# Block state space and attention divided behind its values, in the second mixer of a two-layer block on one Trainium2 core

## The chip, the core and the metric

One core of one Trainium2 chip runs the whole program in one launch. The metric is the device time of one execution in microseconds (us). TensorE (PE), VectorE (DVE), ScalarE (ACT), GpSimd (POOL) and SyncE (SP) run their own instruction lists side by side and wait for each other on semaphores.

## The reference, cut to what matters

`first_block` has two layers, each a mixer and a SwiGLU network; `second_block` follows with two more layers. Everything is float32 on 256 tokens of width 1024. The change is in `first_block`: mostly in layer 1's mixer (`odd_mixer`), which runs a diagonal state space on 256 of its 1024 inner channels (16 groups of 16 channels, 64 complex states a group) beside an attention with 6 heads of width 128.

```python
def s5_ssm(u, a_re, a_im, log_dt, b_re, b_im, c_re, c_im, d_skip, w_glu, b_glu):
    mag = exp(lr * dt); ab = mag * (cos(li * dt) + i sin(li * dt))   # 16 x 64 states
    bu = einsum('bsgh,gph->bsgp', ug, bb)                # drive: complex, 16 -> 64 a group
    x = associative_scan(x[t] = ab * x[t-1] + bu[t])     # over the 256 tokens
    y = einsum(x_re, c_re) - einsum(x_im, c_im) + d_skip * ug
    z = gelu(y)
    return z * sigmoid(z @ w_glu + b_glu)
def mla_attention(...):                                  # 6 heads, causal by chunks of 64
    p = softmax(where(mask, q . k * scale, -inf))        # blocks of 128 queries
    return einsum('bhqk,bkhd->bqhd', p, v)
def odd_mixer(t, ...):
    proj = t @ w_in
    return concatenate([s5_ssm(...), mla_attention(...)]) @ w_out
```

## The kernel before, in words

**Weights.** Every large product is done three times: a weight chunk (128 x 1024 float32, two DMAs of 256 KB by SP into `raw`) is rounded by ACT to `wh` (line 865), POOL forms the rest `wl` in two halves (lines 787, 788), and PE multiplies `wh` by the rounded activations `xh`, `wh` by their rest `xl`, and `wl` by `xh` (lines 2411 to 2413). `raw`, `wh` and `wl` are rings of 6 slots; SP may refill a slot when its chunk is used. The chunks of `w_mod` (the modulation of `second_block`) go straight from `raw` into PE: 8 instructions on four column strips of 32 each (line 2516). They are laid between the steps of `first_block` as `modulate(...)`; twelve pairs stand in the attention loop.

**Order.** Each engine's list is written out by hand; the code's order is the order of the engine. A float32 product leaves two records in the trace, a transpose one.

**First mixer.** DVE's `angles()` reduces the states' angles to one turn (`reduced`, 5 or so small instructions a call) and raises `disc_v`; ACT's exponential (line 1142) waits for it, with attention and convolution queued behind. `discretise()` follows. `state_tables()` makes full tables on DVE in pieces (`yield`) that the first feed-forward network takes between its own instructions: the scaled input matrices, and cosine and sine of every state at each of the 256 tokens.

**Second mixer, PE.** `modulate("mod1_in")` and the turns of the normalised rows (`rows_turn`, line 2574); tile in1; turns of the input matrices (`b_turn`, line 2550) and of u (256 channels by tokens, `ssm_ut`); latent turns (line 2890); the projections uq and ukv with the first drives and states between them; turns of q and k (line 2945; three of them wait for the rotation, `mla_rope`); then the attention loop.

**State space.** The 1024 complex states stand in 8 tiles j of 128. `drive(j)` is two products of 128 x 256 (line 2862), into a bank that DVE multiplies by cosine and sine, scans over 256 tokens and turns back (`state_space`, lines 2017 to 2038); for j of 3 and up POOL does the additions and the turning back. `state(j)` is two products 128 x 256 (line 2870) that add up in one bank; line 2091 adds the skip, ACT takes gelu.

**Attention loop.** Unit u is query block u % 2 of head u // 2. PE: scores of u + 2 (lines 2964, 2965), two modulation chunks, wait `at_p`, one or two transposes of p (line 2986), a drive or a state at odd u, and for odd u from 3 the values of head u // 2 - 1 (lines 2972, 2973), which wait `at_y`, the last head having left `mla_out`. DVE: reciprocal of the row sum (line 2079), maximum of the next unit, and the split of the head's output into `xh` and `xl` (lines 1467, 1469). ACT: p times the reciprocal (line 1275), evacuation of the transposes (line 1281), next exponential (line 1267). Behind the loop stand the values of head 5, `state(7)` and the products of out1 (line 2411).

Of the kernel before, what the change touches and what calls it, by code (L numbers as in the profile page):

```python
# [34 lines left out]
SSM_C, SSM_T, SSM_J = D // 4, (D // 4) // P, 8  # L35
MH, MN, MR, MV = 6, 128, 64, 128
# [8 lines left out]
       ("ln_g", CONV_T), ("ln_b", CONV_T), ("b_glu", SSM_T), ("d_skip", SSM_T), ("a_re", SSM_J), ("a_im", SSM_J),  # L45
# [4 lines left out]
       ("cos_d", 64), ("sin_d", 64), ("cos_x", 64), ("sin_x", 64), ("modsum", 48), ("count", 16)]  # L50
# [23 lines left out]
def constants():  # L74
# [14 lines left out]
    put("count", np.broadcast_to(np.arange(16), (P, 16)))  # L89

# [18 lines left out]
def lay_out(x):  # L109
# [14 lines left out]
    v["b_glu"], v["d_skip"] = cols(x["l1_b_glu"]), cols(x["l1_d_skip"])  # L124
# [10 lines left out]
    def blocks(a):  # L135
        a = np.asarray(a)
        out = np.zeros((2, 64, SSM_J, P), f)
        for g in range(16):
            at = 16 * (g % 8)
            out[g % 2, :, g // 2, at:at + 16] = a[g]  # L140
        return out.reshape(P, SSM_J * P)
# [10 lines left out]
        "b_re": blocks(x["l1_b_re"]), "b_im": blocks(x["l1_b_im"]),  # L152
        "c_re": blocks(np.asarray(x["l1_c_re"]).transpose(0, 2, 1)),
        "c_im": blocks(np.asarray(x["l1_c_im"]).transpose(0, 2, 1)),
# [82 lines left out]
def build(nc, a, out):  # L237
# [61 lines left out]
    POOL_STATES = 3  # L299
# [14 lines left out]
    with ExitStack() as stack:  # L314
# [36 lines left out]
        def view(phase, *shape, at=None):  # L351
# [12 lines left out]
        pc, ps_ = view("ssm", SSM_J, SEQ), view("ssm", SSM_J, SEQ)  # L364
# [19 lines left out]
        bbar = [view("l0", SSM_J, P, at=KEEP + 7296 + i * 1024) for i in range(2)]  # L384
        braw = [view("l0", SSM_J, P, at=KEEP + 4096 + i * 1024) for i in range(2)]
        btmp = [view("l0", SSM_J, P, at=KEEP + 3072), view("l0", SSM_J, P, at=KEEP + 6144)]
        ptmp = view("l0", SSM_J, SEQ, at=KEEP + 4096)
        angle, sin_half, sin_n, cos_n = (bt[0].rearrange("p a b -> p (a b)")[:, 256 * i:256 * i + 256]
                                         .rearrange("p (j n) -> p j n", j=SSM_J) for i in range(4))
        turns_f = bt[1].rearrange("p a b -> p (a b)")[:, 0:256].rearrange("p (j n) -> p j n", j=SSM_J)  # L390
        turns_i = bt[1].rearrange("p a b -> p (a b)")[:, 256:512].rearrange("p (j n) -> p j n", j=SSM_J).bitcast(I32)
# [385 lines left out]
        def _(pool):  # L777
# [20 lines left out]
            def state(j):  # L798
# [4 lines left out]
                if j > POOL_STATES:  # L803
                    pool.wait_ge(x_state, j + j - POOL_STATES)
# [2439 lines left out]
```

## Time and profile before

| | |
|---|---|
| timed executions | 1824.0, 1834.28, 1822.65 us; median 1824.0 |
| profiled execution | 1826.6 us, span 1824.8 us |
| PE busy | 1779.4 us, 98% |
| POOL busy | 1376.5 us, 75% |
| ACT, DVE busy | 903.2 us, 804.2 us |
| DMA moved | 348.28 MB, mean 191 GB/s |
| first feed-forward network | about 130 to 326 us of the span |
| second mixer | about 326 to 453 us, its attention loop 384 to 422 |

Idle time in brackets is that of the engine just before the instruction, with what ended it. Ends of products are modelled, so a PE row may overlap the next: prices come from the chain of waits or from distances of starts.

### The profile page before, as it was taken

The page shows a single profiled execution, that of the slowest core. Times are in us where ns is not written, and L with a number is a line of the kernel's source. Part 1 is how long each engine was busy: PE and PEld are TensorE (multiplying, and loading weights), DVE is VectorE, ACT ScalarE, POOL GpSimd, SP SyncE. Part 2 cuts the span into 40 slices and gives each one's busy share as a digit, 9 for nine tenths or more (in the row PEclk, how much of TensorE's full clock was granted, in tenths as well). Part 3 has the DMA queues.
Part 4 walks back from the last instruction along what each step waited for, and adds up shares of the span by engine and source line. Part 5 has one row for each costly group of instructions (what it writes and reads, how often), then busy time and mean ns, then how long its engine had stood idle before and what let it go on. Part 6 is the DMA issues. An engine that isn't in the chain of part 4 may idle for free.

```text
span 1824.8 us, 28994 instructions
## 1 busy us (share of the span) xinstructions
PE 1779.4 (98%) x9846; PEld 1442.8 (79%) x9846; DVE 804.2 (44%) x1556; ACT 903.2 (49%) x1410; POOL 1376.5 (75%) x811
## 2 busy tenths in 40 slices
PE   9989999998999999999999999999999999999997
PEld 7768888766788887788888977788888987788886
DVE  4565874573455554443112555441114665441112
ACT  6456443645644554555445445554446445554443
POOL 7359997546988779578888884578887894678884
PEclk9999999999999999999999999999999999999999
DMA  7767876688987745346665562356654563346562
GB/s 271 192 196 255 274 245 217 193 280 272 294 273 249 234 139 185 115 137 194 199 189 181 168 190 93 120 158 201 201 184 150 171 209 107 110 148 194 189 189 70
DMA packets 259110, 348.28 MB, mean 191 GB/s; under 512 B 20936, under 2 KB 161608, under 8 KB 259016
## 3 DMA queue, kind: packets, MB, share of 16 engines
q1 hardware_dynamic: 255840, 340.44, 58.4%
q10 hardware_dynamic: 3176, 6.62, 1.3%
q8 instruction: 55, 0.90, 0.2%
q14 instruction: 39, 0.32, 0.1%
HBM read 343.24 MB, written 1.64 MB: 189 GB/s over the span
## 4 chain that ended last, share of the span: by engine, by line
PE 88%; DVE 5%; ACT 2%; issue 1%; DMA 1%; POOL 1%; SPq 0%; DVEq 0%; POOLq 0%; ACTq 0%
PE bank L2411 23%; PE bank L2413 23%; PE bank L2412 22%; PE bank L2550 2%; PE bank L3128 2%; PE bank L2481 1%; PE bank L2480 1%; PE bank L2479 1%; PE bank L3118 1%; PE bank L3167 1%; PE bank L2516 1%; POOL wl L828 1%; PE bank L2783 1%; PE bank L2574 0%; ACT wh L865 0%
## 5 line engine op out<-in xcount | busy, mean ns | idle before, releaser
L828 POOL TENSOR_TENSOR wl<-raw,wh 128x1024 fp32r<-128x1024 f32 x300 | 734.1, 2461 | 102.5 <-ACT wh L1030 79.0
L2411 PE MATMUL bank<-wh,xh 128*128 128x512 f32 (+1 forms) x1590 | 625.4, 393 | 9.6 <-POOL wl L788 2.9
L2413 PE MATMUL bank<-wl,xh 128*128 128x512 f32 (+1 forms) x1590 | 611.4, 385 | 0.0
L2412 PE MATMUL bank<-wh,xl 128*128 128x512 f32 (+1 forms) x1590 | 609.9, 384 | 0.0
L787 POOL TENSOR_TENSOR wl<-raw,wh 128x512 fp32r<-128x512 f32 (+1 forms) x232 | 309.5, 1334 | 286.0 <-ACT wh L865 284.5
L1030 ACT ACTIVATE wh<-raw 128x1024 fp32r<-128x1024 f32 x270 | 286.4, 1062 | 429.0 <-PE bank L2413 411.9
L865 ACT ACTIVATE wh<-raw 128x1024 fp32r<-128x1024 f32 (+2 forms) x268 | 275.6, 1049 | 170.7 <-PE bank L2413 90.1
L2411 PEld LDWEIGHTS bank<-wh,xh 128*128 128x128 f32 x1590 | 299.1, 188 | 73.8 <-issue 8.2
L2413 PEld LDWEIGHTS bank<-wl,xh 128*128 128x128 f32 x1590 | 298.7, 188 | 60.8
L2412 PEld LDWEIGHTS bank<-wh,xl 128*128 128x128 f32 x1590 | 299.5, 188 | 54.8
L788 POOL TENSOR_TENSOR wl<-raw,wh 128x512 fp32r<-128x512 f32 (+1 forms) x232 | 309.6, 1335 | 0.0
L1599 DVE TENSOR_TENSOR arena<-arena,bank 128x256 f32<-128x256 f32 x66 | 24.8, 418 | 323.2 <-ACT arena L1017 323.2
L2411 PE MATMUL bank<-wh,hh 128*128 128x512 f32 x420 | 163.6, 389 | 0.0
L2413 PE MATMUL bank<-wl,hh 128*128 128x512 f32 x420 | 163.5, 389 | 0.0
L2412 PE MATMUL bank<-wh,hl 128*128 128x512 f32 x420 | 163.4, 389 | 0.0
L1602 DVE CAST hh<-bank 128x512 fp32r<-128x512 f32 x55 | 38.0, 691 | 189.8 <-PE bank L2550 189.8
L1923 DVE SCALAR_TENSOR_TENSOR bank<-arena,small,bank 128x256 f32<-128x256 f32 x216 | 86.9, 481 | 11.1 <-DMA arena<-in_w_mod 11.1
L2413 PEld LDWEIGHTS bank<-wl,hh 128*128 128x128 f32 x420 | 78.9, 188 | 16.4
L2412 PEld LDWEIGHTS bank<-wh,hl 128*128 128x128 f32 x420 | 78.9, 188 | 16.3
L2411 PEld LDWEIGHTS bank<-wh,hh 128*128 128x128 f32 x420 | 78.8, 188 | 16.3
L1391 ACT ACTIVATE arena<-bank 128x256 f32<-128x256 f32 (+2 forms) x96 | 41.9, 490 | 97.7 <-PE bank L3128 97.7
L2272 DVE TENSOR_REDUCE small<-bank 128x1 f32<-128x256 f32 (+2 forms) x96 | 50.5, 554 | 82.3 <-PE bank L3118 81.2
(399 smaller groups left out, 2037.3 us busy)
## 6 DMA issues: line engine op xcount, KB each, us to landing
raw<-in_w_ffn_in SPq DMA_DIRECT2D x264, 256.0 KB, 2.9
raw<-in_w_in SPq DMA_DIRECT2D x224, 256.0 KB, 2.9
raw<-in_w_ffn_out SPq DMA_DIRECT2D x132, 256.0 KB, 2.9
raw<-in_w_mod SPq DMA_DIRECT2D x120, 256.0 KB, 4.3
raw<-in_l_w_gate SPq DMA_DIRECT2D x88, 256.0 KB, 3.7
raw<-in_l_w_up SPq DMA_DIRECT2D x88, 256.0 KB, 4.4
raw<-in_l_w_down SPq DMA_DIRECT2D x88, 256.0 KB, 4.1
arena<-in_w_mod SPq DMA_DIRECT2D x36, 512.0 KB, 5.4
```

Of the source, the lines that this page charges most:

```text
L787: nc.gpsimd.tensor_tensor(wl[:, s, 0:h], raw[:, s, 0:h], words(wh)[:, s, 0:h], ALU.subtract)
L788: nc.gpsimd.tensor_tensor(wl[:, s, h:n], raw[:, s, h:n], words(wh)[:, s, h:n], ALU.subtract)\
L828: nc.gpsimd.tensor_tensor(wl[:, s, :], raw[:, s, :], words(wh)[:, s, :], ALU.subtract)\
L865: nc.scalar.activation(wh[:, s, first:n], raw[:, s, first:n], ACT.Copy).then_inc(hi_ready, 1)
L1030: nc.scalar.activation(wh[:, s, :], raw[:, s, :], ACT.Copy).then_inc(hi_ready, 1)
L1391: nc.scalar.activation(pT2[:, e, 0:keys // P, (i % 2) * P:(i % 2) * P + P], unit_bank(u)[:, 0:keys].rearrange("p (a b) -> p a b", b=P), AC ...
L1602: v.tensor_copy(hh[:, :, :], src).then_inc(hid_split, 1)
L1923: ins = v.scalar_tensor_tensor(out=dst, in0=raw_mod[:, k, :], scalar=c, in1=acc, op0=ALU.mult, op1=ALU.add)
L2272: v.tensor_reduce(nmax[:, g % 4:g % 4 + 1], unit_bank(u)[:, 0:keys], AX_X, ALU.max, negate=True)\
L2411: mm(dst, x_hi, w_hi, start=first, stop=False, skip_group_check=True)
L2412: mm(dst, x_lo, w_hi, start=False, stop=False, skip_group_check=True)
L2413: return mm(dst, x_hi, w_lo, start=False, stop=last, skip_group_check=True)
```

## The change

The state space goes over blocks of 4 tokens (`SSM_L`), 64 blocks. Within a block, outputs come from a 128 x 128 matrix for each 32 channels (`near`: powers of the state's factor between B and C, plus the skip), made on PE in 32 x 128 pieces (`near_products`) and completed on DVE (`near_matrix`). Between blocks, B times the powers 3 to 0 (`bpow`) drives one complex state a block; DVE scans 64 blocks for four tiles at once, 256 columns, and C times the powers 1 to 4 (`cpow`) reads it. So there are two calls c = 0, 1 of `drive`, `state` and the DVE chain instead of eight, none of it on POOL. `block_rows` lays u out by place in the block, in place of its four transposes. Inputs `ssm_b`, `ssm_c` (as many bytes as b_re and b_im had) come over ACT's queue; SP's loads of c_re and c_im (512 KB each), with SP's waits for `res_done` and `mod_acc` ahead of in1, are gone.

Attention: p is no longer scaled. The reciprocals of a head's sums are spread over 128 rows by two transposes in `mla_values`; ACT copies the raw output to `q1` (`mla_raw`), DVE multiplies and splits (`mla_divided`).

First mixer: `angles()` reduces one angle more, makes three products of angles, 12 exponents a state and the denominators; ACT's exponential has 96 columns for 8. `step_factors()` (20 or so small instructions) goes behind the copy of the modulation rows, and `state_tables()` has ten pieces.

On PE this is one odd step of the attention loop (u = 3; from its modulation chunks to the next unit's scores), before:

```order
L2516 MATMUL bank<-raw,cw 32x256 x8
L2986 MATMUL bank<-con,arena 128x128 x2
L2862 MATMUL bank<-Y,arena 128x256 x2
L2870 MATMUL bank<-extra,arena 128x256 x2
L2972 MATMUL bank<-arena 128x256
L2973 MATMUL bank<-arena 128x128
```

and now:

```order
L2549 MATMUL bank<-raw,cw 32x256 x8
L3049 MATMUL bank<-con,arena 128x128 x2
L3036 MATMUL bank<-con,small 128x128 x2
L3038 MATMUL bank<-arena 128x256
L3039 MATMUL bank<-arena 128x128
```

The drive (2862) and the state (2870) have left the step, and two transposes of reciprocals (3036) have come in ahead of the values.

PE from the last chunk ahead of the turns of q and k to the turns that wait for the rotation, before:

```order
L2516 MATMUL bank<-raw,cw 32x256 x4
L2862 MATMUL bank<-Y,arena 128x256 x2
L2870 MATMUL bank<-extra,arena 128x256 x2
L2945 MATMUL bank<-con,arena 128x128 x12
L2945 MATMUL bank<-con,Y 128x128 x12
L2516 MATMUL bank<-raw,cw 32x256 x12
L2945 MATMUL bank<-con,xf 128x128 x6
```

and now:

```order
L2549 MATMUL bank<-raw,cw 32x256 x4
L3006 MATMUL bank<-con,arena 128x128 x12
L3006 MATMUL bank<-con,Y 128x128 x12
L2549 MATMUL bank<-raw,cw 32x256 x12
L2931 MATMUL bank<-Y,arena 32x64 x4
L2936 MATMUL bank<-extra,arena 32x63 x8
L2931 MATMUL bank<-Y,arena 32x64 x4
L2936 MATMUL bank<-extra,arena 32x63 x8
L2931 MATMUL bank<-Y,arena 32x64 x4
L2936 MATMUL bank<-extra,arena 32x63 x8
```

`drive(3)` and `state(1)` are gone ahead of the turns; the new `state(0)` (2931, 2936) stands behind them (a fourth such round follows, then the turns from `xf`).

ACT at the end of the loop, from the last two units' p to the gelu, before:

```order
L1275 ACTIVATE arena<-arena,small 128x128
L1281 ACTIVATE arena<-bank 128x128
L1275 ACTIVATE arena<-arena,small 128x256
L1281 ACTIVATE arena<-bank 128x2x128
L865 ACTIVATE wh<-raw 128x1024 x3
L1289 ACT_TABLE_LOAD
L1289 ACTIVATE extra<-extra 128x512
```

and now:

```order
L1254 ACTIVATE arena<-bank 128x256
L1264 ACTIVATE arena<-bank 128x128
L1264 ACTIVATE arena<-bank 128x2x128
L1254 ACTIVATE arena<-bank 128x256 x2
L847 ACTIVATE wh<-raw 128x1024 x3
L1276 ACT_TABLE_LOAD
L1276 ACTIVATE extra<-bank 128x4x64 x2
```

The scalings (1275) are gone; the copies of heads 4 and 5 (1254 x2) now stand ahead of the first casts of out1's weights (847).

```diff
-            nc.scalar.activation(mag, t8a, ACT.Exp).then_inc(disc_a, 1)
+            nc.scalar.activation(mag_pow, mag_arg, ACT.Exp).then_inc(disc_a, 1)
...
-            for i, w in enumerate(("b_re", "b_im")):
-                act.dma_start(braw[i], a[w].rearrange("p (j c) -> p j c", j=SSM_J)).then_inc(b_in, 16)
+            for dst, w in ((b_raw, "ssm_b"), (c_raw, "ssm_c")):
+                act.dma_start(dst, a[w].rearrange("p (n j c) -> p n j c", n=2, j=2 * SSM_J)).then_inc(b_in, 16)
...
+            def mla_raw(h):
+                act.wait_ge(at_pv, h + 1)
+                nc.scalar.activation(q1[:, 0, 0:SEQ], mla_out[:, 0:SEQ], ACT.Copy).then_inc(y_raw, 1)
             mla_exp(0)
...
                                      bank[u % 3][:, 0:n * P].rearrange("p (a b) -> p a b", a=n), ACT.Copy).then_inc(at_ev, 1)
                 if u + 2 < 2 * MH:
                     mla_exp(u + 2)
+                if u >= 3 and u % 2:
+                    mla_raw(h - 1)
+            mla_raw(MH - 1)
...
             hi_until(plan.first["out1"] + RING - 1)
-            act.wait_ge(y_skip, 1)
-            nc.scalar.activation(zv, yv, ACT.Gelu_apprx_tanh).then_inc(z_gelu, 1)
+            act.wait_ge(y_state, SSM_T)
+            for c in range(SSM_T):
+                ins = nc.scalar.activation(zv[:, SEQ * c:SEQ * c + SEQ].rearrange("p (b r) -> p r b", r=SSM_L),
+                                           state_bank[:, SEQ * c:SEQ * c + SEQ].rearrange("p (r b) -> p r b", r=SSM_L),
+                                           ACT.Gelu_apprx_tanh)
+            ins.then_inc(z_gelu, 1)
...
-                step(v.tensor_scalar(th16, th, 16.0, None, ALU.mult))
-                settle()
-                reduced(th16, ki, kf)
-                n = spread(C_("count").unsqueeze(1), SSM_J, 16)
-                step(v.tensor_tensor(angle[:, :, 0:16], n, spread(th.unsqueeze(2), SSM_J, 16), ALU.mult))
-                step(v.tensor_tensor(angle[:, :, 16:], n, spread(th16.unsqueeze(2), SSM_J, 16), ALU.mult))
+                step(v.tensor_scalar(th4, th, float(SSM_L), None, ALU.mult))
+                step(v.tensor_scalar(th64, th, 16.0 * SSM_L, None, ALU.mult))
+                settle()
+                reduced(th4, ki, kf)
+                reduced(th64, ki, kf)
+                for at, n, x, by in ((0, 16, th4, "count"), (16, 4, th64, "count"), (20, 12, th, "powers")):
+                    step(v.tensor_tensor(angle[:, :, at:at + n], spread(C_(by)[:, 0:n].unsqueeze(1), SSM_J, n),
+                                         spread(x.unsqueeze(2), SSM_J, n), ALU.mult))
                 settle()
                 reduced(angle, turns_i, turns_f)
+                step(v.tensor_tensor(mag_arg, spread(C_("powers").unsqueeze(1), SSM_J, 12), spread(t8a.unsqueeze(2), SSM_J, 12), ALU.mult))
                 v.tensor_scalar(angle, angle, 3.1415925, -3.1415925, ALU.min, ALU.max).then_inc(disc_v, 1)
...
+            def step_factors():
...
+            def block_decay(c):
+                by_block = decay.rearrange("p (j b) -> p j b", j=4)
+                step(v.tensor_copy(by_block, spread(mag4[:, 4 * c:4 * c + 4].unsqueeze(2), 4, SSM_N)))
+                settle()
+                step(v.memset(by_block[:, :, 0:1], 0.0))
+            def near_matrix(c):
+                dve.wait_ge(near_mm, c + 1)
+                for jj in range(4):
+                    j = 4 * c + jj
+                    ins = v.scalar_tensor_tensor(out=near[:, j, :], in0=ident, scalar=V_("d_skip", j), in1=scratch[:, P * jj:P * jj + P],
+                                                 op0=ALU.mult, op1=ALU.add)
+                    ins.then_inc(near_set, 1) if jj == 3 else step(ins)
...
             undivided_norm("mix1", "l1_mix_pre", accb)
+            near_matrix(0)
+            block_decay(0)
             take("in1", 0, lambda t, p: v.tensor_scalar(proj[:, t, 0:512], p, back[:, t:t + 1], None, ALU.mult))
...
+            near_matrix(1)
...
-                for j in range(SSM_J):
-                    dve.wait_ge(bu_done, j + 1)
-                    b = drive_bank[j % 2]
-                    cosj, sinj = pc[:, j, :], ps_[:, j, :]
+                for c in range(SSM_T):
+                    dve.wait_ge(bu_done, c + 1)
...
-                        n = j - POOL_STATES
-                        if n:
-                            dve.wait_ge(x_scan, 2 * n)
-                        v.tensor_tensor(two(spun), two(b[:, :]), cos2, ALU.mult).then_inc(bu_taken, 1)
-                        v.tensor_tensor(two(turned), two(b[:, :]), sin2, ALU.mult).then_inc(bu_taken, 1)
-                        yield
...
                     step(v.tensor_tensor(two(spun), two(b[:, :]), cos2, ALU.mult))
                     step(v.tensor_tensor(scanned[:, 0:SEQ], b[:, SEQ:], sinj, ALU.mult))
-                    v.tensor_tensor(scanned[:, SEQ:], b[:, 0:SEQ], sinj, ALU.mult).then_inc(bu_taken, 1)
+                    step(v.tensor_tensor(scanned[:, SEQ:], b[:, 0:SEQ], sinj, ALU.mult))
...
-            for _ in range(5):
+            for _ in range(2):
...
             v.engine_nop().then_inc(mla_rope, 1)
-            for _ in range(3):
-                next(ssm)
...
+            def mla_divided(h):
+                y = mla_out[:, 0:SEQ]
+                dve.wait_ge(y_raw, h + 1)
+                step(v.tensor_tensor(y, q1[:, 0, 0:SEQ], mla_out[:, SEQ:], ALU.mult))
+                settle()
+                split(2 + h, 1, y, at_y)
...
                 v.reciprocal(rinv[:, u % 4:u % 4 + 1], rsum[:, u % 4:u % 4 + 1]).then_inc(at_rinv, 1)
...
+                next(ssm, None)
                 if u >= 3 and u % 2:
                     h = u // 2 - 1
-                    dve.wait_ge(at_pv, h + 1)
-                    split(2 + h, 1, mla_out[:, 0:SEQ], at_y)
...
+            mla_divided(MH - 1)
...
-            ahead_of_norm("mod1_in", "mix1")
+            def near_products(c):
+                if c:
+                    pe.wait_ge(near_set, c)
+                for j in range(4 * c, 4 * c + 4):
+                    for i in range(2):
+                        for q in range(SSM_L):
+                            ins = mm(scratch[32 * q:32 * q + 32, P * (j % 4):P * (j % 4) + P], bpow[i][:, j, SSM_L - 1, :],
+                                     cpow[i][:, j, 3 - q:7 - q, :].rearrange("p d c -> p (d c)"), start=i == 0, stop=i == 1,
+                                     skip_group_check=True)
+                ins.then_inc(near_mm, 1)
+            modulate("mod1_in", slice(0, 2))
+            pe.wait_ge(b_bar, 1)
+            pe.wait_ge(c_pow, 1)
+            near_products(0)
+            rows_turn("mix1", (0, 1))
...
+            def block_rows():
+                for j in range(SSM_J):
+                    for t in range(TT):
+                        at = SSM_N * j + 32 * t
+                        for q in range(SSM_L):
+                            ins = mm(ut_bank[32 * q:32 * q + 32, at:at + 32], proj[:, t, SSM_G * j:SSM_G * j + SSM_G],
+                                     ident.rearrange("p (b s) -> p s b", s=SSM_L)[:, q, :], start=True, stop=True, skip_group_check=True)
+                ins.then_inc(ssm_ut, 1)
+            def drive(c):
+                for jj in range(4):
+                    for i in range(2):
+                        at = SEQ * i + SSM_N * jj
+                        ins = mm(drive_bank[c][:, at:at + SSM_N], bt[i][:, 4 * c + jj, :], uT1[:, c, SSM_N * jj:SSM_N * jj + SSM_N],
+                                 start=True, stop=True, skip_group_check=True)
                 ins.then_inc(bu_done, 1)
-            def state(j):
-                pe.wait_ge(x_state, j + 1 + max(0, j + 1 - POOL_STATES))
-                y = state_bank[:, SEQ * (j // 4):SEQ * (j // 4) + SEQ]
-                for i in range(2):
-                    ins = mm(y, cz[i][:, j, :], z_cos[:, SEQ * i:SEQ * i + SEQ], start=j == 0 and i == 0, stop=j % 4 == 3 and i == 1,
-                             skip_group_check=True)
+            def state(c):
+                pe.wait_ge(near_set, c + 1)
+                pe.wait_ge(x_state, c + 1)
+                for r in range(SSM_L):
+                    at = SEQ * c + SSM_N * r
+                    for jj in range(4):
+                        mm(state_bank[32 * jj:32 * jj + 32, at:at + SSM_N], near[:, 4 * c + jj, SSM_G * r:SSM_G * r + SSM_G],
+                           uT1[:, c, SSM_N * jj:SSM_N * jj + SSM_N], start=True, stop=False, skip_group_check=True)
+                    for i in range(2):
+                        for jj in range(4):
+                            z = SEQ * i + SSM_N * jj
+                            ins = mm(state_bank[32 * jj:32 * jj + 32, at + 1:at + SSM_N], cpow[i][:, 4 * c + jj, 4 + r, :],
+                                     z_cos[:, z:z + SSM_N - 1], start=False, stop=i == 1, skip_group_check=True)
                 ins.then_inc(y_state, 1)
...
+            near_products(1)
+            for b in range(2):
...
+            block_rows()
...
-            state(1)
...
+            state(0)
...
+                pe.wait_ge(at_rinv, 2 * h + 2)
+                for qb in range(2):
+                    at = (2 * h + qb) % 4
+                    tr(mla_out[:, SEQ + qb * P:SEQ + qb * P + P], rinv[:, at:at + 1].broadcast_to([P, P]), ident)
...
-            drive(4)
-            state(2)
-            drive_at, state_at = {1: 5, 3: 6, 5: 7}, {3: 3, 5: 4, 7: 5, 9: 6}
...
-                pe.wait_ge(at_p, u + 1)
+                pe.wait_ge(at_exp, u + 1)
                 for kc in range(1 + u % 2):
...
-                if u in state_at:
-                    state(state_at[u])
+                if u == 6:
+                    state(1)
                 if u >= 3 and u % 2:
...
-            state(7)
```

## Rows read from the trace of the kernel before

**Rows 1.** The page: busy time, share of the span, instructions; chain by engine.
```profile
PE 1779.4 (98%) x9846; PEld 1442.8 (79%) x9846; DVE 804.2 (44%) x1556; ACT 903.2 (49%) x1410; POOL 1376.5 (75%) x811
```

**Rows 2.** Windows: engines busy in each stretch, PEclk, DMA share, GB/s.
```profile
130.00:326.00 196.00, 193.87 (x948) 158.24 (x938) 123.71 (x215) 90.83 (x119) 176.21 (x73) 1.00 0.73 239
...
381.00:424.00 43.00, 37.88 (x319) 24.59 (x317) 29.36 (x75) 16.34 (x51) 29.73 (x37) 1.00 0.87 296
```

**Rows 3.** DVE, ACT, PE timelines, first mixer: start, us, instruction [idle<-releaser].
```profile
83.55 0.57 DVE L1660 SCALAR_TENSOR_TENSOR small<-small 128x8 f32<-128x8 f32 x3
84.15 0.29 DVE L1675 TENSOR_TENSOR arena<-con,small 128x128 f32<-128x128 f32 x1
...
86.72 0.29 DVE L1679 TENSOR_SCALAR arena<-arena 128x256 f32<-128x256 f32 x1
...
87.89 0.22 ACT L1142 ACTIVATE small<-small 128x8 f32<-128x8 f32 x1
...
95.96 1.09 PE L2550 MATMUL bank<-con,arena 128*128 128x128 f32 x8 [0.85 <-DVE arena L1876]
```

**Rows 4.** Chain of waits: start, us, engine, line; PE prices.
```profile
332.71 0.87 PE bank L2574 x8
...
388.08 1.00 PE bank L2516 x16
...
389.45 0.87 PE bank L2862 x4
```

**Rows 5.** Groups of lines, PE: form, records | busy us, mean ns | idle before.
```profile
L3144 PE MATMUL bank<-arena 128*64 128x64 f32 x128 | 5.1, 222 | 0.0
L2542 PE MATMUL bank<-con,rdiag 128*128 128x24 f32 x32 | 3.9, 258 | 0.0
```

**Rows 6.** PE timeline, second mixer: waits of the block state space.
```profile
327.59 1.09 PE L2574 MATMUL bank<-con,X 128*128 128x128 f32 x8 [2.01 <-DVE X L1558]
...
347.04 0.66 PE L2890 MATMUL bank<-con,arena 128*128 128x128 f32 x4 [0.86 <-DVE arena L1979]
...
372.86 1.47 PE L2945 MATMUL bank<-con,arena 128*128 128x128 f32 x12
...
378.12 0.88 PE L2945 MATMUL bank<-con,xf 128*128 128x128 f32 x6 [1.05 <-DVEq L2064]
...
383.75 1.13 PE L2870 MATMUL bank<-extra,arena 128*128 128x256 f32 x4 [1.01 <-DVE extra L2038]
...
386.95 0.70 PE L2964 MATMUL bank<-arena 128*128 128x256 f32 x2 [0.37 <-ACT arena L1281]
...
418.20 0.33 PE L2986 MATMUL bank<-con,arena 128*128 128x128 f32 x1 [0.48 <-ACT arena L1275]
```

**Rows 7.** ACT timeline: last evacuation of the value projection.
```profile
371.37 0.41 ACT L1255 ACTIVATE arena<-bank 128x256 f32<-128x256 f32 x1
```

**Rows 8.** Windows inside the attention loop: DMA share and GB/s.
```profile
415.00:420.00 5.00, 4.52 (x47) 2.86 (x46) 2.41 (x8) 2.09 (x7) 3.88 (x5) 1.00 0.98 341
```

**Rows 9.** PE, ACT, DVE, POOL timelines at the end of the loop.
```profile
419.46 0.44 PE L2986 MATMUL bank<-con,arena 128*128 128x128 f32 x2
419.73 0.60 PE L2972 MATMUL bank<-arena 128*128 128x256 f32 x2
...
420.21 1.05 ACT L865 ACTIVATE wh<-raw 128x1024 fp32r<-128x1024 f32 x1
...
420.59 0.42 DVE L1467 CAST xh<-bank 128x256 fp32r<-128x256 f32 x1 [2.82 <-PE bank L2973]
...
422.63 1.27 POOL L788 TENSOR_TENSOR wl<-raw,wh 128x512 fp32r<-128x512 f32 x1
```

**Rows 10.** Chain of waits: first product of the output GEMM.
```profile
424.04 0.47 PE bank L2411
```

**Rows 11.** Windows around the one stretch at the lower clock.
```profile
104.00:107.50 3.50, 1.62 (x8) 1.00 (x6) 0.00 (x0) 2.00 (x2) 1.76 (x2) 1.00 1.04 383
107.50:111.00 3.50, 3.48 (x9) 2.77 (x10) 0.00 (x0) 0.00 (x0) 1.59 (x2) 0.54 0.92 334
```

More of the change, by code:

```diff
@@ L383, in build @@
         u_copy = nc.dram_tensor("u_copy", (2, 32, 4, 2, PAD + SEQ + 1), F32, kind="Internal").ap()
[L384 to L389, printed above, removed]
@@ L1738, in state_tables @@
                 yield
                 settle()
-                step(v.tensor_tensor(pc, pc, ptmp, ALU.subtract))
+                v.tensor_tensor(bpow_all, bpow_all, t, ALU.add).then_inc(b_bar, 1)
                 yield
-                step(v.tensor_tensor(four(ps_), coarse(sin_n), fine(cos_n), ALU.mult))
-                settle()
+                dve.wait_ge(b_bar, 1)
+                c_far, t = cpow_all[:, :, SSM_L:], blocks(c_tmp, SSM_L)
+                step(v.tensor_tensor(c_far, each(c_raw[:, 0], SSM_L, SSM_G), factors(c_re, SSM_L, SSM_G), ALU.mult))
@@ L2853, in _ @@
             pe.wait_ge(mod_ready, 8)
-            ahead_of_norm("mod1_in", "mix1")
-            def b_turn(b):
-                turn(b_bank[b], lambda i, t: bbar[i][:, 2 * b + t, :], b_tr)
-            def drive(j):
-                if j >= 2:
-                    pe.wait_ge(bu_taken, j - 1 + max(0, j - 1 - POOL_STATES))
-                for i in range(2):
-                    ins = mm(drive_bank[j % 2][:, SEQ * i:SEQ * i + SEQ], bt[i][:, j, :], uT1[:, j // 4, :], start=True, stop=True,
-                             skip_group_check=True)
-                ins.then_inc(bu_done, 1)
@@ L2878, in _ @@
             column_tile("in1", 0, 0, "mix1", rest_of_rows)
-            pe.wait_ge(b_bar, 2)
-            for b in range(3):
+            near_products(1)
+            for b in range(2):
                 b_turn(b)
             tile_chunk("in1", 1, 0)
-            pe.wait_ge(b_ev, 2)
-            b_turn(3)
+            for b in range(2, 4):
+                pe.wait_ge(b_ev, 2 * b - 2)
+                b_turn(b)
             def latent_turn(i):
@@ L2913, in _ @@
             latent_chunk("uq", 2)
-            drive(2)
             x_ready("lat1", 2)
@@ L2918, in _ @@
                 latent_chunk("ukv", i, shift=2)
-                if i == 0:
-                    pe.wait_ge(c_neg, 1)
-                    pe.wait_ge(c_in, 32)
-                    state(0)
-            drive(3)
-            state(1)
             def mla_turn(b):
```

225 lines of the change are left out of this document (114 added, 111 removed).

## The prediction

> **What bounds the kernel now.** The page first [rows 1]: PE is busy for 98% of the span, so only what PE does or waits for is worth anything. The windows [rows 2] (start and end, length, then busy time of PE, PEld, DVE, ACT and POOL with their counts, granted clock, DMA share, GB/s) show where it waits: of the 196 us of the first feed-forward network PE misses 2, of the 43 us of the attention loop 5. All the change's work on POOL, and nearly all on DVE, therefore moves under PE. The first mixer, the second mixer's PE list and the seam between loop and out1 can move the end.
>
> **First mixer.** In `angles()` three of five small instructions of a reduction take 0.57 [rows 3], so one more reduction costs 0.95; with one scaling more (0.19), a third product of angles and the exponents (0.29 at most each, the product of 128 columns) it ends some 1.5 later than 86.72 + 0.29: at 88.5. ACT's exponential started at 87.89 and had waited for nothing, so it comes 0.6 later; 96 columns for 8 cost 0.1 at most. PE waits 0.85 at 95.96 for the DVE work behind that, so I pass the delay on: **+0.6** (bounds 0, if slack on the way takes it, and 1.5). `step_factors()`, 20 instructions of 0.19, is 3.8 us of DVE beside a feed-forward network in which DVE is busy 124 of 196 [rows 2]; the tables there shrink a little. Both 0; were they on the path, 3.8.
>
> **PE's products.** Prices [rows 4, 5]: a drive or a state of before (4 records) takes 0.87; eight transposes 0.87, so 0.11 each; sixteen records on four strips, two rounds of 256 columns, take 1.00, so a round of 128 columns is 0.25 by halving. A round of 64 columns is between 0.125 (halving again) and 0.16 (L3144: 128 records on two strips, 32 rounds, in 5.1 us): I take 0.13. A round of 32 columns lies between 0.0625 and 0.16: 0.1. A product with full 128-column weights and few columns is between 0.11 (a quarter of 0.434) and 0.24 (L2542: 16 instructions in 3.9): I take 0.24, for its shape is nearest.
>
> Removed up to the last transposes of the loop (419.46): 8 drives and 7 states, 13.0, and 4 transposes of u, 0.44. Added: `near_products(1)`, 8 rounds, 2.0; `block_rows`, 16 rounds of 32 columns, 1.6; two drives of 8 products, 3.8; two states of 12 rounds, 3.2; the reciprocals of heads 0 to 3, 8 transposes, 0.87. That is 11.5 (with the rounds and drives at their bounds 8.7 and 13.1): **-2.0**. `near_products(0)`, also 2.0, stands where PE waits 2.01 for DVE at 327.59 [rows 6]: 0; without that cover 2.0.
>
> **PE's waits** [rows 6], each less what now stands ahead of it. The 0.86 at 347.04 is filled by near(1), whose 2.0 I have counted: -0.86. The 1.05 at 378.12: DVE did the chains of three states ahead of the rotation and now does one: -1.05. The 1.01 at 383.75 is for state(2), which is gone: -1.01. The 0.48 at 418.20 is for ACT's scaling, which is gone: -0.48. Waits like the 0.37 at 386.95 stand at the even units; that of the unit behind state(1) is covered: -0.37. Against this, two covers go. The turns at 372.86 had drive(3) and state(1) ahead of them (1.74), while ACT's last copy of the value projection ended at 371.37 + 0.41 = 371.78 [rows 7]; PE would now be there at 371.0: +0.79. At u = 1 no drive covers the softmax any more; of its 0.87 I let half come back: +0.46. Sum of waits **-2.5** (bounds -3.8 and -1.0).
>
> **Supply.** The loop's 24 modulation chunks, less the 6 that the ring holds, are 18 x 0.52 = 9.4 MB; at the 341 GB/s of a window with DMA share 0.98 [rows 8] 27.7 us. PE went from 383.75 to 419.46, 35.7 us, and would now need about 29. Other transfers take a share too, so supply may come out up to 2 short; but 383 GB/s has been seen [rows 11], which would need 24.6. I take **+1.0** (0 to 2.0).
>
> **The seam.** Before [rows 9, 10]: last transposes 419.46, values of head 4 419.73, DVE's cast 420.59, ACT's first cast of out1 420.21, and its first product at 424.04, 3.83 behind that cast (1.05 on ACT, two halves of 1.27 on POOL, hand-overs). All that is 4.58. Now ACT's list has the copies of heads 4 and 5 ahead of the cast, and head 5's needs head 4's split. From the last transposes: values of head 4 end 1.13 later, plus 0.22 of reciprocals, 1.35; ACT copy 0.41 [rows 7] with hand-over, 1.8; multiply, cast, subtract on DVE at 0.46 apiece, 3.2; reciprocals and values of head 5, 1.1, 4.3; its copy, 4.8; then the 3.83: 8.6. So out1 starts **+4.1** later against the last transposes (bounds +2.5, if POOL's lateness is made up in out1's first tile, and +4.6). Queued behind ACT's copy are all casts of out1's chunks, behind those POOL.
>
> **Clock.** PE was busy 1.62 of 3.5 us ahead of 107.5, and in the next 3.5 us the granted clock was 0.54, i.e. 1.2 GHz nearly throughout [rows 11], which costs up to 3.5 x 0.46 = 1.6. In the new seam PE has about 2 of work in 8.6. I expect a fall, partly over idle time: **+1.2** (0 to 1.6).
>
> **Rule against rows.** The trace shows 40 ns a record where 64 columns go over two strips [rows 5] and nothing narrower. The Trainium skill (TensorEngine Tiling (Array Packing), Instruction Overhead) says that a product of one column lasts as long as one of 60, and that nothing is gained by splitting what is already small; (TensorE: Matmul & The Clock Gate, Wait, 56ns, not 53.3ns?) puts a floor of 25 ns between two starts. By it the 128 records of `block_rows` would be an estimated 3.2 for my 1.6 and the 96 of each state 2.4 for 1.6, in all +3.2; no row shows it.
>
> **Sum.** -2.0 - 2.5 + 1.0 + 0.6 + 4.1 + 1.2 = +2.4. The profiled execution took 1826.6 (span 1824.8), so one like it would take 1829.0; it was 2.6 above the median 1824.0 of the timed runs, which is what the forecast is compared with: **1826.4**. With every term at its low bound at once it would be 1818, with every one at its high bound 1832; the forecast's own range is 1821 to 1831.
>
> **Rivals.**
> B, the seam does not grow: POOL and ACT make up their lateness, or the clock stays up. For it: POOL is idle in part [rows 2] and out1's first tile has a modulation chunk between its pieces. Against: the orders are fixed lists, and one head's copy needs the previous head's split. Then -4.5 + 0.6 = -3.9: 1820. Chance 0.2.
> C, small products and supply cost their upper bounds: rounds at 0.16 (+0.7 for the states' 24, +1.0 for the rows' 16), supply 2.0 for 1.0, clock 1.6 for 1.2, waits 0.8 worse: +3.9 on the forecast, so 1830. For it the 0.16 of L3144 and the DMA share of 0.98. Against: 383 GB/s is possible. Chance 0.28.
> D, the other side: strips do not overlap for short products, and each of the 224 small instructions (32 + 32 + 64 + 96) costs 0.24 as one of L2542. That is 53.8 - 2.0 of cover against my 6.8: +45, so 1871. It decides (over 1% slower, 1842) from 0.11 an instruction. Against: L2516 does 8 of 256 columns on four strips in 1.00. Chance 0.04.
> E, the SSM's gain is eaten anyway: DVE's chain for 256 columns is late at state(0) or state(1), each up to 1.0 (the wait of state(2) before). 1828. Chance 0.06.
>
> **How the numbers follow.** Forecast 0.42, B 0.2, C 0.28, E 0.06, D 0.04. About 1% is what a measurement of this kernel can tell from no change: 18 us. Only D is beyond it: slower 0.05. Nothing here can give 18 us, since the whole second mixer's SSM is 13: faster 0.01. The range 1818 to 1834 holds B and C with the spread of single runs.
>
> **What would show it.** Right: state(2)'s and the rotation's waits gone; POOL without `z_cos` work; a new wait of 1.8 or so ahead of the last head's values and one of over 3 ahead of out1's first product; ACT's first cast of out1 over 4 behind the last transposes; granted clock under 1 there; the exponential of the first mixer at 88.5. Wrong: `block_rows` over 3 us, a state over 3, DMA waits of the loop's chunks over 2 us, out1's first product within 6 us of the last transposes, or new waits of b-table turns behind near(1).

## The result

| | before | changed |
|---|---|---|
| timed executions | 20: median 1822.99 us, 1821.06 to 1834.28 | 20: median 1832.09 us, 1825.71 to 1838.46 |
| ratio to before | | 1.0037, 95% interval 1.0024 to 1.005 |
| profiled execution | 1826.6 us, span 1824.8 us | 1828.23 us, span 1826.4 us |

The change makes the kernel slower by 0.24 to 0.5%, some 4 to 9 us; forecast was +2.4. The medians lie 9.1 us apart. The ratio is smaller: it is near that of the means (1.0038), and four of before's 20 executions, at 1831 or more, raise before's mean. The two profiled spans differ by 1.6 only. Two things hide the rest. The profile of before holds a stretch at half clock [rows 11] and a late load in its first mixer; run e4 below keeps the first mixer of before and has neither, so they vary between executions. And the profile of the changed kernel is free of a stall that three more profiles with the same state space will show (e1, e2, f1), and that, by the spread of the times, most of its executions seem to have. The spread is part of the result: the changed kernel's executions cover 13 us.

The late load is in ACT's timeline of the first mixer, first of before, then of the changed kernel:

```profile
105.47 1.06 ACT L865 ACTIVATE wh<-raw 128x1024 fp32r<-128x1024 f32 x1 [3.21 <-DMA raw<-in_l_w_out]
```

```profile
104.05 1.06 ACT L847 ACTIVATE wh<-raw 128x1024 fp32r<-128x1024 f32 x1 [1.15 <-DMA raw<-in_l_w_out]
```

ACT's cast of a chunk of out0 waits for its load in both and comes 1.4 us later in the profile of before (105.47 for 104.05). With the half clock behind it, 1.7 us, this makes 3.1 of the 3.2 us that the changed kernel's profile gains between 100 and 111 us. Another 0.9 us goes the other way later: at 505.98 PE waits 1.38 us for DVE, in before 0.47, and DVE stands behind loads of `w_mod`. This wait is 0.87 in e1 and absent in f1 and f2, so it too varies between executions, and nothing here was run on it.

**The page and the windows of the changed kernel**, answering [rows 1, 2] (window, length, then busy time of PE, PEld, DVE, ACT, POOL with their counts, granted clock, DMA share, GB/s):

```profile
PE 1781.3 (98%) x10270; PEld 1445.5 (79%) x10270; DVE 794.8 (44%) x1568; ACT 900.1 (49%) x1404; POOL 1346.8 (74%) x776
```

```profile
130.00:326.00 196.00, 194.82 (x1000) 159.85 (x996) 128.56 (x233) 90.28 (x118) 172.90 (x74) 1.00 0.73 235
...
381.00:424.00 43.00, 34.41 (x391) 21.84 (x390) 19.46 (x65) 16.80 (x48) 5.95 (x5) 0.95 0.90 318
424.00:453.00 29.00, 27.17 (x147) 19.23 (x145) 6.55 (x11) 13.15 (x22) 14.78 (x13) 0.96 0.63 207
```

PE is about as busy as before (1781.3 us for 1779.4), with 424 records more. POOL's 29.73 us in the loop's window are 5.95 now. The granted clock of 0.95 in the loop's window is new: in [rows 2] it is 1.00.

**PE's timeline of the changed kernel in the second mixer** (start, busy us, instruction; in brackets idle time ahead of it and what ended it), answering [rows 6]:

```profile
322.73 1.93 PE L2893 MATMUL bank<-arena 128*32 128x128 f32 x64
324.91 1.09 PE L2607 MATMUL bank<-con,X 128*128 128x128 f32 x8 [0.26 <-DVE X L1548]
...
339.00 1.95 PE L2893 MATMUL bank<-arena 128*32 128x128 f32 x64
...
345.88 2.12 PE L2913 MATMUL bank<-con,arena 128*32 128x32 f32 x128
...
352.21 2.00 PE L2921 MATMUL bank<-Y,arena 128*128 128x64 f32 x16
...
371.87 1.53 PE L3006 MATMUL bank<-con,arena 128*128 128x128 f32 x12 [0.73 <-ACT arena L1236]
...
375.95 0.30 PE L2931 MATMUL bank<-Y,arena 128*32 128x64 f32 x8
...
377.40 0.87 PE L3006 MATMUL bank<-con,xf 128*128 128x128 f32 x6
...
386.19 0.49 PE L3026 MATMUL bank<-arena 128*128 128x128 f32 x2 [0.47 <-ACT arena L1264]
```

Lines 2893 (`near_products`), 2913 (`block_rows`), 2921 (drive) and 2931 (the first of a state's four rounds) are the new products. `near_products(0)` fits into the old wait of 2.01 and leaves 0.26 of it. The waits of 0.86 at the latent turns, 1.05 at the rotation and 1.01 at a state are gone; 0.73 at 371.87 and 0.47 at 386.19 are the two covers that went.

**The seam in the changed kernel**, PE and ACT, answering [rows 9, 10]:

```profile
411.70 0.64 PE L2549 MATMUL bank<-raw,cw 128*32 128x256 f32 x8 [0.60 <-DMA raw<-in_w_mod]
412.27 0.44 PE L3049 MATMUL bank<-con,arena 128*128 128x128 f32 x2
...
412.76 0.60 PE L3038 MATMUL bank<-arena 128*128 128x256 f32 x2
...
415.48 0.40 PE L3036 MATMUL bank<-con,small 128*128 128x128 f32 x2 [1.90 <-issue]
...
420.69 0.76 PE L2444 MATMUL bank<-wh,xh 128*128 128x512 f32 x1 [4.15 <-POOL wl L798]
```

```profile
413.62 0.38 ACT L1254 ACTIVATE arena<-bank 128x256 f32<-128x256 f32 x1 [0.49 <-PE bank L3039]
416.58 0.38 ACT L1254 ACTIVATE arena<-bank 128x256 f32<-128x256 f32 x1 [2.58 <-PE bank L3039]
416.86 1.99 ACT L847 ACTIVATE wh<-raw 128x1024 fp32r<-128x1024 f32 x2
```

Last transposes at 412.27, the values of head 4 at 412.76, ACT's copy of head 4 at 413.62, of head 5 at 416.58, only then the first cast of out1, and its first product at 420.69: 8.42 us behind the transposes for 4.58 before, with PE idle 1.90 and 4.15. The clock answers:

```profile
419.30:426.20 6.90, 5.51 (x16) 3.93 (x20) 0.00 (x0) 3.45 (x4) 6.19 (x6) 0.51 0.24 83
453.40:456.90 3.50, 3.50 (x25) 1.81 (x22) 2.97 (x5) 3.45 (x6) 3.25 (x4) 0.51 0.89 250
```

In the first window PE's work on the first quarter of out1's tile and the modulation chunk behind it goes from 420.69 to 426.66, 5.97 us; before it went from 424.04 to 427.53, 3.49 us. The low clock costs 2.5 us there. The second window stands behind a wait of PE of 1.83 us at the start of the second feed-forward network, which before had as well, at the full clock; it costs 1.0 us more.

### The profile page after: what moved, and what is told of

It reads as the page before. It is cut to its first block, busy times and chain, and to the rows that moved or that the text cites. A ratio compares the mean times of both kernels' runs of the same rounds, so it can differ in the third digit from the quotient of the medians.

```text
span 1826.4 us, 29796 instructions
## 1 busy us (share of the span) xinstructions
PE 1781.3 (98%) x10270; PEld 1445.5 (79%) x10270; DVE 794.8 (44%) x1568; ACT 900.1 (49%) x1404; POOL 1346.8 (74%) x776
## 4 chain that ended last, share of the span: by engine, by line
PE 88%; DVE 4%; ACT 3%; POOL 1%; issue 1%; DMA 1%; SPq 0%; ACTq 0%; POOLq 0%; DVEq 0%
PE bank L2444 23%; PE bank L2446 23%; PE bank L2445 23%; PE bank L2583 3%; PE bank L3188 2%; PE bank L2514 1%; PE bank L2513 1%; PE bank L2512 1%; PE bank L3178 1%; PE bank L3227 1%; PE bank L2549 1%; POOL wl L810 1%; PE bank L2607 1%; DVE X L1548 0%; ACT wh L847 0%
```

## The experiments

Beside these runs the kernel before had medians of 1824.17 (31 executions, runs e1 to e4) and 1823.63 us (35 executions, runs f1 to f4). Runs of different groups are best compared by their distance from these.

### e1_after_again: the changed kernel once more

> The changed kernel once more, for a second profile and a second comparison with the kernel before. Two theories run through these runs. Theory S (seam): what costs is the end of the attention loop, where ACT's copies of heads 4 and 5 stand ahead of the first casts of out1 (first product 8.4 us behind the last transposes instead of 4.6), and the granted clock falls in the idle time there; the block state space itself gains about 4.5. Theory B (blocks): the block state space costs in most executions, by its many short products or by the longer start in the first mixer, and the seam is a minor matter. Both expect here 1829 to 1833 us, 6 to 9 over the kernel before. S: a stretch at half clock behind the seam in this profile too, the interval from last transposes to out1's first product 8.4. B: low clock or lost time also in the first mixer or around the short products.

Median 1833.79 us (1826.25 to 1842.66, 9 executions), ratio 1.005 (1.0029 to 1.0071), 0.8 above the range that both theories gave. The seam was as in the first profile, 8.42 us from the last transposes (418.94) to out1's first product (427.36), with a stretch at half clock behind it; out1's first quarter took 5.40 us. The low stretch at 453 is missing here, though the wait of 1.83 ahead of it is not. But this span is 1831.1, and a second stretch stands at 155, behind a stop of PE that neither theory had:

```profile
157.29 1.11 PE L2583 MATMUL bank<-con,arena 128*128 128x128 f32 x4 [4.38 <-DVE arena L1586]
```

```profile
155.00:161.90 6.90, 4.61 (x13) 3.83 (x14) 5.59 (x14) 2.95 (x3) 3.54 (x3) 0.51 0.37 130
424.60:431.40 6.80, 4.04 (x10) 3.20 (x11) 0.41 (x1) 4.39 (x5) 6.68 (x6) 0.50 0.38 133
```

PE waits 4.38 us for DVE early in the first feed-forward network. DVE comes out of `step_factors()`, 18 small instructions. These are its rows and POOL's at that time:

```profile
142.19 1.31 DVE L1722 TENSOR_TENSOR arena<-arena,small 128x32 f32<-128x32 f32 x1
...
146.03 2.30 DVE L1727 COPY arena<-arena 128x32 f32<-128x32 f32 x1
148.25 2.44 DVE L1712 TENSOR_SCALAR arena<-arena 128x32 f32<-128x32 f32 x1
150.61 2.43 DVE L1730 COPY arena<-arena 128x32 f32<-128x32 f32 x1
152.96 2.38 DVE L1712 TENSOR_SCALAR arena<-arena 128x32 f32<-128x32 f32 x1
155.26 0.17 DVE L1730 COPY arena<-arena 128x32 f32<-128x32 f32 x1
```

```profile
144.66 1.29 POOL L798 TENSOR_TENSOR wl<-raw,wh 128x512 fp32r<-128x512 f32 x1
145.91 9.40 POOL L810 TENSOR_TENSOR wl<-raw,wh 128x1024 fp32r<-128x1024 f32 x4
```

An instruction on 128 x 32 numbers takes 1.2 to 1.3 us, then 2.3 to 2.4. POOL's rows are halves of chunks of 1.28 and, in one row of four, whole chunks of 9.40 / 4 = 2.35, starting at 145.91, 148.26, 150.61 and 152.96. DVE's slow instructions start at 146.03, 148.25, 150.61 and 152.96 and end with them; when POOL pauses at 155.31, the next takes 0.17. In the first profile of the changed kernel the longest of the 18 are the last two:

```profile
146.25 4.89 DVE L1733 COPY arena<-arena 128x256 f32<-128x256 f32 x2
```

So in the two profiles DVE and POOL interleave differently: the 18 instructions took 10.8 us in the first profile of the changed kernel (140.37 to 151.14), 15.5 here (140.42 to 155.91), and 3.4 would be 18 of 0.19. The slack that hides them ends near 151, so the first case costs nothing and the second 4.7 us and, with the clock that falls in the stop, some 6.5: the offset between the two profiles is 0 up to 149 us and 6.5 at 162.

### e2_casts_first: out1's first casts ahead of the raw copies

```diff
+                if u == 2 * MH - 1:
+                    hi_until(plan.first["out1"] + 1)
                 if u >= 3 and u % 2:
                     mla_raw(h - 1)
+            hi_until(plan.first["out1"] + 3)
             mla_raw(MH - 1)
```

> The changed kernel with ACT's cast of out1's first chunk ahead of the copy of head 4, and two more casts ahead of the copy of head 5; nothing else moved. Theory S: out1's first product comes 4.7 to 5.5 us behind the last transposes instead of 8.4, no idle stretch over 2.5 us in the seam, so 3 to 3.5 less idle and 2.5 less at half clock: 1823 to 1826 us. Theory B: 1828 to 1831, since at best the 3.5 of the seam come back.

Median 1826.81 us (1820.77 to 1831.14, 12 executions), ratio 1.0003 (0.9986 to 1.002): 7.0 less than e1 (two runs of 9 and 12 executions). PE's timeline:

```profile
419.83 0.44 PE L3052 MATMUL bank<-con,arena 128*128 128x128 f32 x2
...
423.62 0.40 PE L3039 MATMUL bank<-con,small 128*128 128x128 f32 x2 [2.48 <-issue]
...
424.66 0.47 PE L2447 MATMUL bank<-wh,xh 128*128 128x512 f32 x1
```

The first product comes 4.83 behind the last transposes (419.83 to 424.66), and there is no low clock from 410 to 460. This run's profile still has the stop at 156 and its 15.5 us of `step_factors()`. The median came out 0.8 above theory S's 1823 to 1826.

### e3_blocks_only: the block state space with the old attention

```diff
+                act.wait_ge(at_rinv, u + 1)
+                nc.scalar.activation(p1[:, u % 3, 0:keys], p1[:, u % 3, 0:keys], ACT.Copy, scale=rinv[:, u % 4:u % 4 + 1])\
+                  .then_inc(at_p, 1)
...
-                    mla_raw(h - 1)
-            mla_raw(MH - 1)
```

> The changed kernel with the attention as before: p scaled on ACT ahead of its transposes, no transposes of reciprocals, no raw copies, the head's output split straight from its bank. The block state space stays. Theory S: the last transposes come 3 to 4 us earlier than before, the seam is 4.6 long or shorter, no stretch at half clock there: 1817 to 1820 us, faster than the kernel before by 0.2 to 0.3%. Theory B: 1827 or more.

Median 1826.23 us (1820.09 to 1831.34, 12 executions), ratio 0.9998 (0.9976 to 1.002). Theory S's 1817 to 1820 was missed by 6, and theory B's "1827 or more" nearly hit. Yet the profiled execution is one of the best (span 1818.3), shows no low clock at all but at the end of the program, and has this seam:

```profile
412.26 0.44 PE L3038 MATMUL bank<-con,arena 128*128 128x128 f32 x2
...
416.85 0.47 PE L2437 MATMUL bank<-wh,xh 128*128 128x512 f32 x1 [1.54 <-POOL wl L798]
```

4.59 us, as expected. The executions fall in two groups, 1820.1 to 1821.3 (three) and 1825.3 to 1831.3 (nine). The profile, with 10.8 us of `step_factors()`, is of the first. So S was right on the seam and incomplete: the two groups suggest a second cost of 5 us or more in most executions of this kernel. Theory L, below, was made for it.

### e4_division_only: the kernel before with the new division

> The kernel before with the division moved behind the values alone (two transposes of reciprocals a head, raw copy on ACT, multiplication on DVE), and the old state space. Theory S: +0.9 of transposes, -0.5 of the wait for the scaling, +3.8 of the seam, and 1.7 to 3.4 for a fall of the clock: 1828 to 1831 us. Theory B: 1823 to 1825.

Median 1831.64 us (1829.37 to 1842.74, 11 executions), ratio 1.0049 (1.0027 to 1.0071), with the old state space and no `step_factors()`:

```profile
416.11 0.44 PE L3001 MATMUL bank<-con,arena 128*128 128x128 f32 x2
...
424.84 0.47 PE L2422 MATMUL bank<-wh,xh 128*128 128x512 f32 x1 [3.28 <-POOL wl L789]
```

8.73 us between last transposes and first product, and low clock at 426 and at 457. The division alone therefore costs 7.5 us by the medians, 0.6 more than theory S's range. Its profile shows where: the seam is 4.1 longer, out1's first quarter takes 5.07 for 3.49 us, the fall at 457 costs about 1 and the way to the last transposes 0.3. Theory B's 1823 to 1825 is out.

### f1_seam_filled: PE kept busy in the seam

```diff
+            keep_pace(8, bank[4])
             mla_values(MH - 1)
+            keep_pace(18, bank[4])
             pe.wait_ge(at_ev, 2 * MH)
```

> The changed kernel with products on constants (128 x 128, float32, into a free bank) in the seam: 8 of them (1.7 us) before the values of head 5, 18 (3.9 us) behind them, where PE waited 1.9 and 4.2. They add nothing to the result. Theory S (the seam's idle time brings the clock down): no stretch at half clock from 410 to 460, out1's first product where it was (8.4 to 8.6 behind the last transposes), and the four first pieces of out1 take 5.8 instead of 8.3: 1829 to 1831 us against 1833.8 of the changed kernel. Rival (the clock falls by itself, whatever PE does there): low stretches stay, 1833 to 1835.

Median 1829.28 us (1824.7 to 1833.79, 12 executions), ratio 1.0016 (0.9996 to 1.0035).

```profile
420.69 0.44 PE L3049 MATMUL bank<-con,arena 128*128 128x128 f32 x2
...
421.84 1.95 PE L2538 MATMUL bank<-ones 128*128 128x128 f32 x16
...
424.80 4.18 PE L2538 MATMUL bank<-ones 128*128 128x128 f32 x36
429.13 0.47 PE L2444 MATMUL bank<-wh,xh 128*128 128x512 f32 x1
```

```profile
420.00:437.00 17.00, 16.62 (x118) 13.29 (x119) 2.56 (x6) 8.44 (x11) 9.98 (x8) 1.00 0.68 245
453.00:464.00 11.00, 8.88 (x68) 6.05 (x64) 8.29 (x14) 9.26 (x20) 5.09 (x4) 1.00 0.77 239
```

The first product comes 8.44 behind the transposes, as in the changed kernel; the filling (line 2538) gains nothing there. But the clock stays at 1.00, the first quarter of out1's tile with its modulation chunk takes 3.48 us (429.13 to 432.61) for 5.97, and there is no low stretch at 453 (nor was there in e1). The expectation's 5.8 for these pieces was a wrong count; its comparison, 2.5 less, is what was measured. Against e1 the median is 4.5 us lower. By their distances from the kernel before, 5.7 here and 9.1 and 9.6 for the changed kernel, it is 3.5 to 4. That is the price of the low clock in this seam by the medians, with ratios whose intervals overlap (0.9996 to 1.0035 and 1.0029 to 1.0071); the rows show less: out1's first quarter gives 1.6 (e4) to 2.6 (f2, below), and 1.9 in e1, whose profiled span is 2.1 longer than this run's. It comes on top of the 3.8 by which the seam is longer.

### f2_factors_from_psum: the same small instructions, read from PSUM

```diff
+                for dst, src in ((pw_re, lam_re[:, :, 1:9]), (pw_im, lam_im[:, :, 1:9]), (t_cos, cos_n[:, :, 0:20]),
+                                 (t_sin, sin_n[:, :, 0:20])):
+                    step(v.tensor_copy(dst, src))
...
-                    signed(c_re[:, :, 0:SSM_L], half, lam_re[:, :, 1:1 + SSM_L], sign)
+                    signed(c_re[:, :, 0:SSM_L], half, pw_re[:, :, 0:SSM_L], sign)
```

`pw_re`, `pw_im`, `t_cos` and `t_sin` lie in `scratch`, a bank of PSUM (the memory that PE writes its products to; the other tiles lie in SBUF) that is free at this time; the intermediate products go there too. There are 22 instructions (the expectation counted 24).

> The changed kernel with the 18 instructions of step_factors at their old place, but reading their tables from a PSUM bank (four copies first, 24 instructions in all). Theory L (lock): in the profiles so far these instructions took 1.2 to 2.4 us where POOL was busy, each ending with a POOL instruction, since they read and write SBUF alone; with one input in PSUM most of them take 0.2, all 24 end within 6 us of their start, and the stop of 4.7 us at 153 to 158 with the low clock behind it is gone: 1827 to 1829 us against 1833.8. Rival W (they wait for something else at this place, a semaphore or a load): they stay at 1.2 to 2.4, 1832 to 1834.

Median 1826.85 us (1825.26 to 1841.8, 12 executions), ratio 1.0026 (1.0005 to 1.0047); ten of the twelve lie between 1825.3 and 1828.2, just about the expected 1827 to 1829. DVE and POOL:

```profile
140.97 0.80 DVE L1717 COPY bank<-arena 128x64 f32<-128x64 f32 x4
...
142.59 0.75 DVE L1730 COPY arena<-bank 128x256 f32<-128x256 f32 x2
...
144.32 0.18 DVE L1743 SCALAR_TENSOR_TENSOR arena<-bank,arena 128x32 f32<-128x32 f32 x1
147.99 0.38 DVE L1942 TENSOR_TENSOR mod<-bank,vec 128x6 f32<-128x6 f32 x4 [3.49 <-PE bank L2584]
```

```profile
141.42 1.30 POOL L797 TENSOR_TENSOR wl<-raw,wh 128x512 fp32r<-128x512 f32 x1 [1.22 <-ACT wh L847]
142.67 1.28 POOL L798 TENSOR_TENSOR wl<-raw,wh 128x512 fp32r<-128x512 f32 x1
```

Four more instructions, and all take 3.53 us (140.97 to 144.50) with POOL at work, for 10.8 or 15.5. DVE now waits for PE at 147.99. Theory L holds, W is out: what made them slow is where they read, not where they stand. The seam and its low clock are still there (8.42 us, out1's first quarter 6.13), which is why this kernel stays above before. There is no low stretch at 453.

### f3_blocks_psum and f4_casts_psum: both repairs

> The block state space with the attention of before (as e3_blocks_only) and step_factors reading from PSUM. Theories S and L together: last transposes 4.5 earlier, seam 4.6, no stop at 153: 1819 to 1821.5 us with little spread, 0.15 to 0.25% faster than the kernel before. Rival W: 1825 to 1828 with the spread of e3_blocks_only (1820 to 1831).

Median 1820.7 us (1819.13 to 1836.3, 12 executions), ratio 0.999 (0.9968 to 1.0012): e3 with the factors from PSUM, 5.5 us below e3 (5.0 by the distances from before), ten of twelve between 1819.1 and 1823.1, the others 1828.9 and 1836.3. The median is 2.9 below before's 1823.63; the interval of the ratio still holds 1, so "faster than before" is likely and not shown.

> The whole change, with out1's first casts ahead of the last two raw copies (as e2_casts_first) and step_factors reading from PSUM. Theories S and L: 1820 to 1822.5 us, so with both repairs the division behind the values costs no more than 1 us against f3_blocks_psum. Rival: 1825 or more, if the division costs elsewhere too.

Median 1822.41 us (1820.18 to 1831.28, 12 executions), ratio 0.9993 (0.9976 to 1.001). With both repairs the division costs 1.7 us against f3, where "no more than 1" was expected; with this spread the two can't be told apart, and no gain of the division is seen.

### What adds up

| kernel | median, us | less the median of before beside it | `step_factors()` in the profile, us | last transposes to out1, us |
|---|---|---|---|---|
| before | 1823.0, 1824.2, 1823.6 | | none | 4.58 |
| changed, first | 1832.1 | +9.1 | 10.8 | 8.42, low clock |
| changed, e1 | 1833.8 | +9.6 | 15.5 | 8.42, low clock |
| e4 | 1831.6 | +7.5 | none | 8.73, low clock |
| f1 | 1829.3 | +5.7 | 15.5 | 8.44, full clock |
| f2 | 1826.9 | +3.2 | 3.5 | 8.42, low clock |
| e2 | 1826.8 | +2.6 | 15.5 | 4.83 |
| e3 | 1826.2 | +2.1 | 10.8 | 4.59 |
| f4 | 1822.4 | -1.2 | 3.5 | 4.59 |
| f3 | 1820.7 | -2.9 | 3.5 | 4.58 |

By these distances seam and clock cost 6.5 to 7 us (the changed kernel less e2), the factors 6 to 6.4 (less f2), and without both costs the block state space alone (f3, with the old attention) stands 3 under before. Together -3 + 7 + 6 = 10, for 9.1 and 9.6 measured, which agrees within what medians of 9 to 20 executions with this spread can tell.

## Why the prediction was right or wrong

| step | forecast | measured |
|---|---|---|
| `near_products(1)` | 2.0 | 1.9 (339.00 to 340.88) |
| `block_rows` | 1.6 | 2.05 (345.88 to 347.93) |
| two drives | 3.8 | 3.5 (352.21 to 354.02; 357.13 to 358.84) |
| two states | 3.2 | 2.9 (375.95 to 377.40; 398.98 to 400.45) |
| waits gone | 0.86, 1.05, 1.01, 0.48, 0.37 | all gone |
| waits come | 0.79, 0.46 | 0.73, 0.47 |
| supply | +1.0 | 0.60 at 411.70 |
| from the turns at 327.59 [rows 6] to the last transposes | -3.5 | -4.51 (91.87 before; 324.91 to 412.27, 87.36; 87.3 to 87.9 in the seven other profiles with block state space) |
| seam | 8.6 | 8.42 |
| clock | +1.2 | 2.5 behind the seam, 1.0 more at 453; 3.5 to 4 by the medians of f1 |
| `step_factors()` | 0 | 0 in this profile, 6.5 in e1's, about 6 by f2 |
| first mixer | +0.6 | +0.5 |

**Right**: the second mixer, within 1 us in all. The prices of the products, measured from start to start as the forecast's were, came out within 0.3 us for three of four, and the exception is `block_rows`, 0.45 dearer: a round of 32 columns took 0.128 (2.05 over 16) and one of 64 columns 0.12 (1.45 over 12), so halving stops there. The Trainium skill (TensorEngine Tiling (Array Packing), Instruction Overhead) says that a product of one column lasts as long as one of 60; the trace agrees so far as 32 columns cost no less than 64. The floor of 25 ns between two starts that the Trainium skill gives in TensorE: Matmul & The Clock Gate (Wait, 56ns, not 53.3ns?) would have made it 3.2, an estimate. On four strips the trace does not show it: 128 records in 2.05 are 16 ns each. The exponential of the first mixer:

```profile
87.98 0.28 ACT L1124 ACTIVATE arena<-arena 128x96 f32<-128x96 f32 x1 [0.35 <-DVE arena L1672]
```

It now waits 0.35 for DVE and comes 0.48 later against PE's own times, as forecast.

**Wrong in size: the clock.** The step "I expect a fall, partly over idle time: +1.2 (0 to 1.6)" took one stretch of 3.5 us, as [rows 11] showed it. In this seam the clock stayed low for 6.8 us, beginning at 419.3, 1.4 ahead of the products, and 5.5 of it was work. The second fall, at 453, came behind the wait of 1.83 for the rows of the second feed-forward network. That it has to do with the seam is not shown: behind the same wait e4 has one too, but so has f4 (at 449), whose seam is short, while e1 and f2, with the long seam and low clock, have none.

**Wrong: `step_factors()` at 0.** The step was "20 instructions of 0.19, is 3.8 us of DVE beside a feed-forward network in which DVE is busy 124 of 196". The cover was looked up in a mean over 196 us, and the price in a place where POOL rested. At its own place POOL works without a pause, and the price is that of POOL's instruction, not DVE's. The bound "on the path, 3.8" was too low as well: measured 10.8 to 15.5. The Trainium skill (SBUF — State Buffer, Who interferes with whom) has this rule: a DVE instruction with two inputs in SBUF, or a copy in a mode that uses both ports, needs the ports it shares with GpSimd and waits for the whole of a running GpSimd instruction; with one SBUF input, outside these modes, it does not. The traces agree on both halves: 2.30 to 2.44 us for 0.17 of work in e1, and 0.18 to 0.20 in f2. The forecast left it out, though POOL's busy time of 176 in the same 196 us stood in [rows 2].

**The range** 1818 to 1834 held the time, in part by luck: the forecast's own range, 1821 to 1831, did not hold the median 1832.1, and by the prediction's sum 1832 needed every term at its high bound, while in truth most terms came out as forecast and one that it had at nothing took 6. The rival C (1830) was nearest in number but for the wrong reasons: neither the short products nor the supply cost what it said. The likeliest case, 1826.4, was off by 5.7 because one named risk was undersized and one term was missing.

**Open.** Four of 20, seven of 31 and seven of 35 executions of the kernel before lie at 1831 to 1837, and the experiments have a few such too; no profile of before caught one. Why DVE and POOL fall into the 10.8 or the 15.5 pattern was not tried, and how often each comes up is only read from the spread of the times: five profiles with the slow factors hold two of 10.8 and three of 15.5. What brings the fall at 453 is open too.

## What to carry to other kernels

Price small VectorE instructions by what GpSimd does in the same microseconds, not by their length: if both read SBUF, each may cost one GpSimd instruction; let one input come from PSUM. Where a copy is added to an in-order engine ahead of casts that feed the next stage, put the casts first: here three lines gave back 6.5 to 7 us. Add the clock to the price of any new idle time ahead of dense products, here some 2 to 4 us for a seam that is 3.8 longer.

## What the runs showed of the hardware that had not been expected

- VectorE instructions of 128 x 32 numbers took 2.30 to 2.44 us instead of 0.17, each ending with the GpSimd instruction that ran (e1), and 0.18 with an input in PSUM (f2).
- A stretch at half clock lasted 6.8 us behind a seam of 8.4 us with 2.4 of PE's work in it (the changed kernel, e1), and as long behind the stop of 4.38 (e1). Others lasted 3.4, that behind e4's seam of 8.7 among them. With the seam filled (f1) there was none.
- Products on four column strips cost 16 ns a record at 32 columns (128 records in 2.05 us).
